# Layer one's q, k and z transposed in 32x32 squares on VectorE and moved by DMA, and the last PLE chunk computed last

## What is computed

```python
def stick_breaking_layer(x, w_in, w_out):
    q, k, v, z = jnp.split(x @ w_in, 4, axis=-1)
    o = stick_breaking_attention(split_heads(q), split_heads(k), split_heads(v))
    return (merge_heads(o) * jax.nn.silu(z)) @ w_out
...
        x = layer_norm(DEEPNORM_ALPHA * x + y, ln_g[i], ln_b[i])
        x = x + (p[i] @ w_ple[i]) * jax.nn.sigmoid(x @ w_ple_gate[i])
```

## Time and profile before

| what | value |
|---|---|
| time, median of 3 runs | 1171.24 us (1170.37 to 1171.37) |
| profiled execution: its time | 1170.72 us |
| its span (first to last instruction or landing) | 1168.8 us |
| PE busy | 1161.9 us, 99% |
| DVE busy | 740.9 us, 63% |
| ACT busy | 591.1 us, 51% |
| PE in the chain that ended last | 95% |
| SP's DMA queue (q1) | 209.74 MB, 57.7% of 16 engines |
| granted clock of PE | 1.0 in the whole run |

### The profile page before, as it was taken

The page is one execution under the profiler, slowest core; times in us unless marked ns, Lnnn a source line. Parts: engine busy times, 40 slices in busy tenths (PEclk is TensorE's granted clock), DMA queues, the critical chain, the costliest instruction groups (busy, mean ns, idle before and its releaser), DMA issues.

```text
span 1168.8 us, 15615 instructions
## 1 busy us (share of the span) xinstructions
PE 1161.9 (99%) x5484; PEld 971.4 (83%) x5484; DVE 740.9 (63%) x786; ACT 591.1 (51%) x669; POOL 21.3 (2%) x43
## 2 busy tenths in 40 slices
PE   9999999999999999999999999999999999999998
PEld 7888888888888888888888888888888888888886
DVE  6765556556556556688777665446677666656863
ACT  6665465456446543455444445544555545435541
...
GB/s 307 287 161 178 181 162 178 179 181 161 165 194 156 241 253 200 137 184 237 232 198 162 197 180 182 193 181 164 169 155 178 167 244 175 252 195 112 211 252 41
DMA packets 112618, 221.49 MB, mean 189 GB/s; under 512 B 6929, under 2 KB 8977, under 8 KB 112065
## 3 DMA queue, kind: packets, MB, share of 16 engines
q1 hardware_dynamic: 110032, 209.74, 57.7%
...
...
## 4 chain that ended last, share of the span: by engine, by line
PE 95%; DVE 2%; DMA 1%; ACT 1%; issue 0%; SPq 0%; ACTq 0%; DVEq 0%
PE acc L1077 29%; PE acc L1079 29%; PE acc L1078 29%; PE aux L1104 2%; PE aux L1121 2%; DVE w_lo L676 1%; PE aux L1145 1%; DVE stage L870 1%; PE aux L1159 1%; DMA raw<-in_w_ple_gate 1%; PE aux L1308 0%; DMA raw<-in_w_in_a 0%; DVE act L691 0%; PE aux L1079 0%; PE aux L1078 0%
## 5 line engine op out<-in xcount | busy, mean ns | idle before, releaser
L676 DVE TENSOR_TENSOR w_lo<-raw,w_hi 128x1024 fp32r<-128x1024 f32 x388 | 471.7, 1224 | 358.5 <-ACT w_hi L417 357.2
L417 ACT ACTIVATE w_hi<-raw 128x1024 fp32r<-128x1024 f32 x388 | 409.7, 1060 | 471.3 <-PE acc L1079 424.5
L1077 PE MATMUL acc<-w_hi,act 128*128 128x512 f32 x1552 | 611.9, 394 | 0.2 <-DVE w_lo L767 0.2
L1079 PE MATMUL acc<-w_hi,act 128*128 128x512 f32 x1552 | 605.1, 390 | 0.0
L1078 PE MATMUL acc<-w_lo,act 128*128 128x512 f32 x1552 | 604.1, 389 | 0.0
L1079 PEld LDWEIGHTS acc<-w_hi,act 128*128 128x128 f32 x1552 | 291.3, 188 | 61.8
L1077 PEld LDWEIGHTS acc<-w_hi,act 128*128 128x128 f32 x1552 | 291.5, 188 | 58.6 <-issue 1.0
L1078 PEld LDWEIGHTS acc<-w_lo,act 128*128 128x128 f32 x1552 | 291.7, 188 | 58.1
L430 ACT ACTIVATE act<-stage 128x1024 fp32r<-128x1024 f32 (+1 forms) x12 | 12.7, 1061 | 33.8 <-DVE stage L870 33.8
L513 ACT ACTIVATE heads<-aux,neg_max 128x128 f32<-128x128 f32 (+1 forms) x32 | 13.0, 419 | 23.7 <-DVE neg_max L1000 23.7
L691 DVE TENSOR_TENSOR act<-stage,act 128x1024 fp32r<-128x1024 f32 (+1 forms) x12 | 14.7, 1226 | 14.3 <-ACT act L430 14.3
...
...
## 6 DMA issues: line engine op xcount, KB each, us to landing
...
```

The source lines that it names most:

```text
L417: nc.scalar.activation(w_hi[:, r], raw[:, r % RAWS], ACT.Copy).then_inc(hi_ready, 1)
L676: nc.vector.tensor_tensor(w_lo[:, r], raw[:, r % RAWS], w_hi[:, r].bitcast(F32), ALU.subtract) \
L1077: nc.tensor.matmul(dst, hi, w_hi[:, r, i], start=begin, stop=False)
L1079: mm = nc.tensor.matmul(dst, lo, w_hi[:, r, i], start=False, stop=end)
```

## The change

**q, k and z of layer one.** DVE's evacuation becomes `nc.vector.transpose` from PSUM to SBUF: each 32x32 square is transposed where it stands (`turn_squares`). To finish a transpose of 128x128 the squares must also change places across partitions. SP does that with 16 DMAs of 32 partitions by 256 elements (32 KB) from `big0` to `heads` (`exchange`), for each q, k and z: four behind each of the loads 3, 4, 5 and 6 of a chunk, the first four behind a wait for DVE's transpose. `q_exchange` stands in the loads of the v chunk, `k_exchange` in those of the z chunk, `z_exchange` in those of the next k chunk (the last one in the output projection). In all that is 12 exchanges and 192 DMAs. ACT's copies and the silu wait for the exchange and read `heads` instead of `aux`. q's first copy covers 1024 elements instead of 512. `q_turn`, `k_turn` and `z_turn` are gone from PE.

**PLE's last chunk.** In layer two PE computes three PLE chunks ahead of the gate. The fourth comes after the last gate piece (`last_ple_product`), in three parts: token tile 0, then each half of the columns of tile 1. ACT keeps a copy of p for it (`keep_p`, 1024 elements). DVE multiplies from PSUM and adds part by part, and SP stores three parts instead of two.

```diff
-            def load_chunk(n, base, matrix, c):
+            def load_chunk(n, base, matrix, c, after=None):
                 for j in range(PC):
                     load(n + j, (base + j) % SPLITS, matrix, j, c)
+                    for step in (after or {}).get(j, ()):
+                        step()
+
+            def exchange(turned, count, dst, src, moved, group):
+
+                if group == 0:
+                    sp.wait_ge(turned, count)
+                rows = slice(group * SQUARE, (group + 1) * SQUARE)
+                for g in range(NS):
+                    sp.dma_start(dst[g * SQUARE:(g + 1) * SQUARE, group * HT // NS:(group + 1) * HT // NS],
+                                 src[rows, g * HT // NS:(g + 1) * HT // NS]).then_inc(moved, 16)
+
+            def q_exchange(c, first=PC // 2 - 1):
+                return {first + i: [lambda i=i: exchange(chunk_evac, c + 1, heads[:, HT:2 * HT], qn, q_moved, i)]
+                        for i in range(NS)}
+
+            def k_exchange(c, first=PC // 2 - 1):
+                return {first + i: [lambda i=i: exchange(chunk_evac, c + 1, heads[:, 0:HT], kn, k_moved, i)]
+                        for i in range(NS)}
...
                 n = g * (4 * PC) + 2 * PC
-                load_chunk(n, 0, wa, g + 2 * G)
-                load_chunk(n + PC, 0, wa, g + 3 * G)
+                load_chunk(n, 0, wa, g + 2 * G, q_exchange(g * 4))
+                load_chunk(n + PC, 0, wa, g + 3 * G, k_exchange(g * 4 + 1))
...
+                load_chunk(n + 3 * PC, 0, wa, g + 1 + G, z_exchange(g * 4 + 3))
+            load_chunk(N_OUT[0] - 2 * PC, 0, wa, 3 * G - 1, q_exchange(4 * G - 4))
+            load_chunk(N_OUT[0] - PC, 0, wa, 4 * G - 1, k_exchange(4 * G - 3))
...
+            load_out_ple_gate(0, w_out_a[0], z_exchange(4 * G - 1, PC + PC // 2 - 1))
...
+            load_out_ple_gate(1, w_out_b[0], {})
+            load(N_LAST, N_LAST % SPLITS, w_ple[1], 0, G - 1)
...
+            for i, (t, lo, hi) in enumerate(LAST_PARTS):
+                sp.wait_ge(x2_ready, 2 * G + i)
+                sp.dma_start(out[t * P:(t + 1) * P, (G - 1) * COLS + lo:(G - 1) * COLS + hi],
+                             columns(res[1], G - 1)[:, t, lo:hi]).then_inc(out_stored, 16)
+            sp.wait_ge(out_stored, 16 * (G - 1 + len(LAST_PARTS)))
...
             def q_copies(k):
 
-                act.wait_ge(qT_psum, k + 1)
-                nc.scalar.activation(qT[:, :, P:T], aux_kt[0][:, :, P:T], ACT.Copy, scale=SCALE).then_inc(qT_ready, 1)
-                nc.scalar.activation(q_parts[:, 0], aux_kt[0], ACT.Copy, scale=SCALE).then_inc(q_hi, 1)
+                act.wait_ge(q_moved, k * MOVED + MOVED)
+                nc.scalar.activation(by_square(q_scaled), qT_x, ACT.Copy, scale=SCALE).then_inc(qT_ready, 1)
+                nc.scalar.activation(by_square(q_parts[:, 0]), qT_x, ACT.Copy, scale=SCALE).then_inc(q_hi, 1)
 
             def k_copies(k):
 
-                act.wait_ge(kT_psum, k + 1)
-                nc.scalar.activation(kT[:, :, P:T], aux_kt[1][:, :, P:T], ACT.Copy).then_inc(kT_ready, 1)
-                nc.scalar.activation(k_parts[:, 0], aux_kt[1][:, :, 0:P], ACT.Copy).then_inc(k_hi, 1)
+                act.wait_ge(k_moved, k * MOVED + MOVED)
+                nc.scalar.activation(by_square(k_own), kT_x[:, 1::TT], ACT.Copy).then_inc(kT_ready, 1)
+                nc.scalar.activation(by_square(k_parts[:, 0]), kT_x[:, 0::TT], ACT.Copy).then_inc(k_hi, 1)
...
             def silu_z_group(k):
                 act.wait_ge(act_ready, k + S_OUT[0])
-                silu_z(k, gt, aux[:, :].rearrange("p (b s n) -> p b s n", b=2, s=2)[:, :, 1])
+                act.wait_ge(z_moved, k * MOVED + MOVED)
+                nc.scalar.activation(by_square(sz_a), gt_x, ACT.Silu).then_inc(sz_ready, 1)
...
+            def keep_p():
+
+                act.wait_ge(p_ready, LAYERS)
+                act.wait_ge(piece_used, N_PLE[1])
+                nc.scalar.activation(p_last, p_act.bitcast(F32), ACT.Copy).then_inc(p_kept, 1)
...
-                pieces(n, n, count=G, before={
-                    0: ple_step[0:1] + [lambda r=r: normalise(2 * layer, r, r) for r in x1]
-                    + ple_step[1:2] + full_step[0:1] + ple_step[2:3] + full_step[1:2] + ple_step[3:4],
-                    2: full_step[2:3]})
+                turns = {0: ple_step[0:1] + [lambda r=r: normalise(2 * layer, r, r) for r in x1]
+                         + ple_step[1:2] + full_step[0:1] + ple_step[2:3] + full_step[1:2] + ple_step[3:G - layer]}
+                turns |= {1: full_step[2:3], 2: [keep_p]} if layer else {2: full_step[2:3]}
+                pieces(n, n, count=G - layer, before=turns)
...
+                    pieces(n + (G - 1) * PC, n, count=1)
                     for t in range(TT):
-                        act.wait_ge(*((tile_0_done, LAYERS + 1) if t == 0 else (piece_used, PIECES)))
+                        act.wait_ge(*((tile_0_done, LAYERS + 1) if t == 0 else (piece_used, N_LAST)))
...
+            def turn_squares(n_end, parity, dst):
+
+                dve.wait_ge(piece_used, n_end)
+                nc.vector.transpose(dst.rearrange("q (p h t c) -> q t h p c", p=NS, h=HG, t=TT),
+                                    acc_of(parity).rearrange("q t (h p c) -> q t h p c", p=NS, h=HG)) \
+                    .then_inc(chunk_evac, 1)
...
             def queries_lo(k):
                 dve.wait_ge(q_hi, k + 1)
-                nc.vector.scalar_tensor_tensor(out=q_parts[:, 1], in0=aux_kt[0], scalar=SCALE,
-                                               in1=q_parts[:, 0].bitcast(F32), op0=ALU.mult, op1=ALU.subtract) \
+                dve.wait_ge(qT_ready, k + 1)
+                nc.vector.tensor_tensor(q_parts[:, 1], q_scaled, q_parts[:, 0].bitcast(F32), ALU.subtract) \
                     .then_inc(q_lo, 1)
 
             def keys_lo(k):
                 dve.wait_ge(k_hi, k + 1)
-                nc.vector.tensor_tensor(k_parts[:, 1], aux_kt[1][:, :, 0:P], k_parts[:, 0].bitcast(F32),
-                                        ALU.subtract).then_inc(k_lo, 1)
+                nc.vector.tensor_tensor(by_square(k_parts[:, 1]), kT_x[:, 0::TT],
+                                        by_square(k_parts[:, 0]).bitcast(F32), ALU.subtract).then_inc(k_lo, 1)
...
+            def squares_end(n, parity, dst):
+                return {PC - 1: [lambda: turn_squares(n + PC, parity, dst)]}
...
-                pieces(n + 2 * PC, 0, gate_steps(g) | chunk_end(n + 2 * PC, 0, qn))
...
-                pieces(N_PLE[layer], N_PLE[layer], count=G,
-                       before={0: turned[1], 2: turned[2]})
+                pieces(N_PLE[layer], N_PLE[layer], count=G - layer,
+                       before={0: turned[1], 2 - layer: turned[2]})
...
+                    pieces(n + c * PC, n, count=1)
                     gain_and_offset(layer, c)
-                    dve.wait_ge(ple_evac, 2 * G)
                     dve.wait_ge(x1_ready, 2 * G)
-                    for t in range(TT):
-                        r, gate = columns(res[1], c)[:, t], stage_tn[:, t]
+                    for i, (t, lo, hi) in enumerate(LAST_PARTS):
+                        r, gate = columns(res[1], c)[:, t, lo:hi], stage_tn[:, t, lo:hi]
                         dve.wait_ge(sig_ready, 2 * G + t)
-                        nc.vector.tensor_tensor(gate, gate, columns(ple[1], c)[:, t], ALU.mult) \
-                            .then_inc(chunk_evac, 1)
-                        dve.wait_ge(chunk_evac, C_GATE[1] + G + t)
+                        dve.wait_ge(last_ple, i + 1)
+                        nc.vector.tensor_tensor(gate, aux_b[:, i, lo:hi], gate, ALU.mult).then_inc(last_product, 1)
+                        dve.wait_ge(last_product, i + 1)
                         nc.vector.tensor_tensor(r, r, gate, ALU.add).then_inc(x2_ready, 1)
...
-            def q_turn(k, c):
-                pe.wait_ge(chunk_evac, c + 1)
-                if not isinstance(k, int) or k > 0:
-                    pe.wait_ge(gated, k)
-                transposes(qn, aux_kt[0], qT_psum)
-
-            def k_turn(k, c):
-                pe.wait_ge(chunk_evac, c + 1)
-                transposes(kn, aux_kt[1], kT_psum)
...
             def key_scores(k, b):
 
+                if not isinstance(k, int) or k > 0:
+                    pe.wait_ge(gated, k)
...
-                    mm = nc.tensor.matmul(s[:, T:SC], kT[:, h, P:T], qT[:, h, P:T], start=False, stop=True,
+                    mm = nc.tensor.matmul(s[:, T:SC], k_own[:, h], q_scaled[:, h, P:T], start=False, stop=True,
...
-            def z_turn(k, c):
-
-                pe.wait_ge(chunk_evac, c + 1)
...
+                for c in range(G - layer):
                     n = N_PLE[layer] + c
...
+                if layer:
+                    turn(2)
                 n, c0 = N_GATE[layer], C_GATE[layer]
                 pe.wait_ge(ple_evac, layer * G + G - 1)
                 chunk(n, n, act0, 0, c0, quarters=s, after={1: [lambda: turn(3)]})
```

(18 more changed lines are left out.)

85 lines of the change are left out of this document (45 added, 40 removed).

## The result

The changed kernel takes 1219.06 us (median of 4 runs, 1217.7 to 1219.92) against 1171.07 us (4 runs) of the kernel before: a ratio of 1.041, 95% interval 1.0392 to 1.0428. It is 48 us slower. The forecast was 1173.4 us and its range ended at 1181.5. The profiled execution took 1217.7 us, its span is 1215.8 us.

The account below looks back on a forecast made before the run. The prediction took PE's instruction stream as the bound: -10.6 us for transposes, +12.8 for waits in `key_scores`, -0.5 and +0.5 for PLE's last chunk gave +2.2, so 1173.4 us, range 1165.5 to 1181.5.

Parts of the forecast that it names:

- -10.6 us for twelve blocks: PE in layer one: dropping the transposes of q, k and z in four groups gains 0.887 us per block.
- Back-to-back issues are 0.44 us apart: SP's queue: price per move, putting the issue of k's sixteenth move in group 1 at 160.95.
- Landing 2.1: A 32 KB move's landing time, taken from the shortest 128 KB load; bounds 0.4 and 3.9 us.
- q's moves end 0.1 us past the time ACT asks for them: 0: ACT behind piece 4 of the k chunk: q's moves cost nothing, as `key_scores` needs q a whole chunk later.
- hold ACT and DVE for about 5 us, again under the eight pieces: 0: Behind piece 2 of the next q chunk: z's moves cost nothing, as PE has eight pieces of split weights ahead.
- The next gate of that wait is the output projection's twelfth piece: 0: Output projection: the hold by z's moves next meets PE at the twelfth piece there and costs 0 us.
- SP's issue time: 0, apart from the delay already counted: Layer one's loads: the 192 moves take 84 us of SP's issue time, at no further cost.
- The rival of the clock: PE falls to about half rate behind each `key_scores` wait, losing 1.8 us more four times: 1180.6 us; chance 0.10.
- I add 0.15: `key_scores`: 0.15 us per wait for weights PE cannot prefetch, making 3.05 us into 3.2 per group.
- The rival of the weights: Held queues use up the eight pieces of lead, so PE also waits for `w_lo`: +8 us, 1181.4; chance 0.05.
- The tail: Layer two's end: 4.95 us from last gate matmul to DVE's last add, against 2.54 before.
- The signs of being wrong: No PE wait in `key_scores`, that wait over 5 us, or matmuls slower than 0.227 us behind it.

Follow-up runs that it names:

- The version without waits: Changed kernel, but k transposed by PE as before and the moves of q and z issued by GpSimd instead of SP: 1163.44 us, ratio 0.9936.
- The one on two queues: Changed kernel, but GpSimd issues q's, z's and half of k's moves, SP k's other half in one row; DVE transposes k before `queries_lo`: 1162.74 us.
- The run with k alone: Changed kernel, but only k goes by DVE's transpose and SP's moves; q and z are transposed by PE as before: 1200.3 us, ratio 1.0247.
- the run with later use: Changed kernel with q's copies behind piece 7 instead of 4, silu and gate behind 6 and 7 instead of 2 and 3: 1208.41 us.
- the long holds: Kernel before the change, with DVE making the low part of k eleven times in a row instead of once: 1194.69 us, ratio 1.0202.
- The short hold: Kernel before the change, with DVE making the low part of k seven times in a row instead of once: 1176.07 us, ratio 1.0045.
- the run with PLE alone: Kernel before with only the change to PLE's last chunk; q, k and z still transposed on PE: 1170.45 us, ratio 0.9996.

## Why the prediction was wrong

- **The bound: right.** PE's stream was the time, and what left it was gained: 1162.74 us where the waits are out of the way, 8.1 us under before.
- **-10.6 us for twelve blocks: right.** The version without waits gained 7.4 of 7.6 us for eight blocks and PLE. The one on two queues gained 8.1 of 11.1 for twelve, with a wait of 1.9 and its fall of 1.6 in its profile.
- **DVE's transpose at the price of the copy: right.** 1.24 us against 1.22 assumed; the upper bound of twice that was far off.
- **"Back-to-back issues are 0.44 us apart": wrong, and the first step that failed.** A move takes SP 0.61 us, four with a load 3.13. The forecast tied only the last four to load 6 and found the two limits "nearly meet" at 160.3 and 160.95. With 0.61 the queue is the later one: 11.3 us from the transpose's end to the start of the last issue, not 8.6. A step of 3.13 us against PE's 2.72 also means that this queue falls behind as long as it moves. The price was taken from loads of the start, and a move that spans 32 partitions was given the same one without a bound above it. The run with k alone measures this term, with the landing's 0.4 in it: 23.8 us of waits for 12.2.
- **Landing 2.1: a little short, copies and `keys_lo` 1.96: right.** The last move of k lands 2.3 us behind the start of its issue in the change and 2.5 with k alone, in group 1; copies and `keys_lo` take 1.9. In the change load 6, issued 0.43 us ahead of the last four moves, lands at 181.45 (3.9 us), and the four take 3.4, 3.0, 2.6 and 2.3 us. With k alone the first four moves, whose load is 1.0 us ahead, take 2.6, 2.3, 2.0 and 1.9. In these rows small moves land later behind a load that is just ahead. The Trainium skill, DMA: Bandwidth & Descriptors, section Queues, rings and completion order, lets a DMA's semaphore step land only after every earlier write of the same engine. The last move lands 0.6 us behind load 6, so the trace is in keeping with it, but does not show that this order is the reason.
- **"q's moves end 0.1 us past the time ACT asks for them: 0" and z "hold ACT and DVE for about 5 us, again under the eight pieces: 0": wrong, the second step.** They were priced against the weights' lead alone. What stands behind them on DVE is k's own transpose, which has no lead. With q late it started 3 us later (5.9 us behind its chunk's end in group 1, 2.6 with k alone), and PE's 6 us of wait became 8.5 to 9.2, 14.3 in group 0. In all this is the larger error: 41.0 us of waits in `key_scores` against 23.8 with k alone. In groups 1 to 3 it comes through ACT and DVE, whose rows show them standing for q and then working off three splits. In group 0 late weights have a part in it, as the run with later use shows.
- **"The next gate of that wait is the output projection's twelfth piece: 0": wrong.** It cost 6.0 us once, and all but 0.7 of it was gone when the silu stood four pieces later. The forecast held z's hold against the lead of eight pieces and left out that the loads stop with it: those that came next ran beside GpSimd's two of 1 MB and took over 11 us.
- **"SP's issue time: 0, apart from the delay already counted": wrong.** On GpSimd's queue the same moves cost half the wait.
- **The rival of the clock: right in kind, at 0.10.** The rows of the start gave 1.8 us per wait, and it is 1.7 to 2.6 in the change, and 1.5 to 3.0 in the long holds: 10.8 of the 47 us. "The waits are shorter than that stretch" spoke against it, but the waits were 8 to 14 us, and one of 1.88 sufficed. The forecast's own 3 us lies between waits of 2.6, of which one in four brought the clock down, and 3.7, which did. So even there the term belonged into the range four times.
- **"I add 0.15" per wait for weights that aren't prefetched:** it had no row behind it. The short hold has 0.8 us over four waits in which the clock stayed up, so 0.2 each.
- **The rival of the weights: not as told.** PE never waited for weights in layer one. Late weights acted through DVE's order: what PE waited for stood behind a split that was late, in the output projection and in group 0.
- **The tail: right,** 4.90 us for 4.95. The lost cover in layer two was given 0.5 and PE has no wait there, at the lower bound. The sum of these terms is too small for the run with PLE alone to tell.
- **The signs of being wrong:** two of the three that the prediction named came, a wait over 5 us and matmuls slower than 0.227 us behind it.
